# Feed-forward blocks of a streaming encoder: high and low x as one moving operand of 1152 columns, in pieces of 384

## The reference, cut to what matters

```python
def sq_relu_ffn(x, w1, w2):                       # w1 1024 x 4096, w2 4096 x 1024
    return jnp.square(jax.nn.relu(x @ w1)) @ w2
...
        x = layer_norm(DN_ALPHA * x + mix, ln1_g[i], ln1_b[i])
        x = layer_norm(DN_ALPHA * x + sq_relu_ffn(x, ffn_w1[i], ffn_w2[i]), ln2_g[i], ln2_b[i])
```

## Time and profile before

| | |
|---|---|
| median of 3 runs | 1731.77 us (1729.48 to 1733.89) |
| the profiled execution | 1733.15 us |
| its span, first to last instruction | 1731.4 us |
| PE busy, share of the span | 1698.0 us, 98% |
| DVE, POOL, ACT busy | 959.6, 910.5, 463.5 us |
| granted TensorE clock, mean | 0.994 |

### The profile page before, as it was taken

One profiled execution on the slowest core, in us unless ns is written; L12 is line 12 of the kernel. 1 busy time (PEld: TensorE's weight loads), 2 busy tenths in 40 slices (PEclk: granted clock), 3 DMA queues, 4 the chain that ended last, 5 costly groups with the idle time before them and its releaser, 6 DMA issues.

```text
span 1731.4 us, 31956 instructions
## 1 busy us (share of the span) xinstructions
PE 1698.0 (98%) x12276; PEld 1631.5 (94%) x12276; DVE 959.6 (55%) x1657; ACT 463.5 (27%) x812; POOL 910.5 (53%) x744
## 2 busy tenths in 40 slices
PE   7999999999999999999999899999999999999996
PEld 7899999999999999999999777999999999999996
DVE  7799999998846451222315822887355431312226
ACT  2344334444213440211202511211024320302105
POOL 6454344444455555555555555445555565555552
PEclk9999999999999999999999999999999999999998
DMA  4223222233122222222222222122222222222221
GB/s 171 80 98 98 98 95 83 79 98 108 59 87 77 82 85 85 77 82 86 85 82 77 94 100 73 65 78 66 86 74 86 84 75 85 85 85 75 84 86 67
DMA packets 45564, 148.03 MB, mean 85 GB/s; under 512 B 7200, under 2 KB 12704, under 8 KB 44320
## 3 DMA queue, kind: packets, MB, share of 16 engines
q1 hardware_dynamic: 37456, 131.09, 22.7%
q10 hardware_dynamic: 8016, 15.59, 2.8%
HBM read 141.50 MB, written 5.15 MB: 85 GB/s over the span
## 4 chain that ended last, share of the span: by engine, by line
PE 70%; DVE 2%; ACT 1%; issue 0%; ACTq 0%; DVEq 0%
PE ps L581 21%; PE ps L582 21%; PE ps L583 21%; PE ps L826 2%; PE ps L827 2%; PE ps L828 2%; PE ps L867 1%; DVE s L1568 0%; PE ps L868 0%; DVE hl L1668 0%; DVE r L1662 0%; PE ps L869 0%; DVE vm L1853 0%; ACT r L1150 0%; DVE na L1723 0%
## 5 line engine op out<-in xcount | busy, mean ns | idle before, releaser
L510 POOL TENSOR_TENSOR wl<-wraw,wh 128x1024 fp32r<-128x1024 f32 x240 | 590.1, 2459 | 20.0
L581 PE MATMUL ps<-xh,wh 128*128 128x288 f32 (+1 forms) x1968 | 588.3, 299 | 9.4 <-DVE xl L1268 9.4
L582 PE MATMUL ps<-xl,wh 128*128 128x288 f32 (+1 forms) x1968 | 585.2, 297 | 0.0
L583 PE MATMUL ps<-xh,wl 128*128 128x288 f32 (+1 forms) x1968 | 585.1, 297 | 0.0
L581 PE MATMUL ps<-hh,wh 128*128 128x288 f32 x1632 | 482.6, 296 | 0.0
L583 PE MATMUL ps<-hh,wl 128*128 128x288 f32 x1632 | 480.8, 295 | 0.0
L582 PE MATMUL ps<-hl,wh 128*128 128x288 f32 x1632 | 480.5, 294 | 0.0
L507 POOL TENSOR_TENSOR tick<-tick 128x1 f32<-128x1 f32 x240 | 59.3, 247 | 761.9 <-DMA wraw<-wstream 761.9
L581 PEld LDWEIGHTS ps<-xh,wh 128*128 128x128 f32 x1968 | 374.3, 190 | 10.1 <-DVE wl L1265 7.9
L583 PEld LDWEIGHTS ps<-xh,wl 128*128 128x128 f32 x1968 | 373.2, 190 | 0.0
L582 PEld LDWEIGHTS ps<-xl,wh 128*128 128x128 f32 x1968 | 372.9, 189 | 0.2
(11 more groups left out here) (226 smaller groups left out, 1713.5 us busy)
## 6 DMA issues: line engine op xcount, KB each, us to landing
wraw<-wstream SPq DMA_DIRECT2D x241, 512.0 KB, 3.4
acb<-acum_scratch ACTq DMA_DIRECT2D x8, 1152.0 KB, 6.1
xr<-x SPq DMA_DIRECT2D x4, 576.0 KB, 7.2
out_y<-r SPq DMA_DIRECT2D x8, 288.0 KB, 2.2
hs<-ssm_in ACTq DMA_DIRECT2D x8, 128.0 KB, 5.8
out_ssm_s<-hsn ACTq DMA_DIRECT2D x8, 128.0 KB, 5.0
out_ssm_p<-hp ACTq DMA_DIRECT2D x8, 128.0 KB, 1.9
bb<-bias_v ACTq DMA_DIRECT2D x1, 1024.0 KB, 4.9
```

What stands on the lines that cost most here:

```text
L510: pool.tensor_tensor(m.wl[:, s], m.wraw[:, s], m.wh[:, s], ALU.subtract).then_inc(S.w_ready, 1)
L581: mm(out, w_hi, x[0], start=start, stop=False)
L582: mm(out, w_hi, x[1], start=False, stop=False)
L583: return mm(out, w_lo, x[0], start=False, stop=stop)
```

## The change

High and low x are laid out side by side in one tensor (`x2`, `h2`), so that a matmul can run from the end of the high part on into the low part. For each step k of a unit there are five matmuls in place of six (`wide_products`): with the high weights over high and low x (1152 columns, 1156 in an up block) in pieces of 384, of 2 x 192 (2 x 194 in an up block: the rest of the high part and the beginning of the low part, to two places of one bank) and of 384; then with the low weights over high x in pieces of 384 and 192 (194). The number of columns is the same. A slot takes three banks (0 to 2, or 3 to 5); the columns of the high product lie side by side in it, and those of the low product too, and the one who empties it adds both: two DVE operations in place of one in a down block (`wide_add`), and in an up block two and a small one for the extra columns (`cda` on ACT, `cd` on DVE). The units that run in halves (the first of a feed-forward, the last two or four) keep the three matmuls of 288 columns; `residual_add` stays for the units outside the feed-forwards. Sums over the partitions move to other banks, and after the first unit the PE waits for `d_mean`, since the next unit writes the banks that the sums are in.

```diff
-        self.xh_ext = put("xh", [P, KT, TX], F32R)
-        self.xl_ext = put("xl", [P, KT, TX], F32R)
+        self.x2_ext = put("x2", [P, 2, KT, TX], F32R)
+        self.xh_ext = self.x2_ext[:, 0]
+        self.xl_ext = self.x2_ext[:, 1]
...
-        self.hh = put("hh", [P, 16, T], F32R)
-        l0 = self.at
-        self.hl = put("hl", [P, 16, T], F32R)
+        l0 = h0 + 16 * T * 4
+        self.h2 = put("h2", [P, 2, 16, T], F32R)
+        self.hh = self.h2[:, 0]
+        self.hl = self.h2[:, 1]
...
+def half_bank(n, s, h):
+
+    return (3 if n % 2 else 2) * s + h
+
+
+def first_bank(n, s, h):
+
+    return (2 if n == 1 else 3) * s + h
+
+
+def sum_banks(n):
+
+    return (4, 6) if n == 1 else (0, 6)
+
+
+def wide_slot(m, s):
+
+    return m.ps[:, 3 * s:3 * s + 3, :].rearrange("p b t -> p (b t)")
+
+
+def high_part(m, s, n=T):
+
+    at = 512 - WIDE
+    return wide_slot(m, s)[:, at:at + n]
...
+def low_part(m, s, width, n=T):
+
+    at = 1024 - (width - WIDE)
+    return wide_slot(m, s)[:, at:at + n]
...
+def twice(ap, step):
+
+    return bass.AP(tensor=ap.tensor, offset=ap.offset, ap=[ap.ap[0], (step, 2), ap.ap[1]])
...
+    def wide_products(s, w, k, x):
+
+        w_hi, w_lo = m.wh[:, w, k * P:(k + 1) * P], m.wl[:, w, k * P:(k + 1) * P]
+        n = x.shape[-1] - WIDE
+        first, last = k == 0, k == KT - 1
+        head, tail, low = m.ps[:, 3 * s, 512 - WIDE:512], m.ps[:, 3 * s + 1, 0:n], m.ps[:, 3 * s + 2, 0:WIDE]
+        x_head, x_tail = x[:, 0, k, 0:WIDE], x[:, 0, k, WIDE:WIDE + n]
+        mm(head, w_hi, x_head, start=first, stop=False)
+        mm(twice(tail, 512 - n), w_hi, twice(x_tail, x[:, :, k, :].ap[1][0] - WIDE), start=first, stop=False)
+        mm(low, w_hi, x[:, 1, k, n:n + WIDE], start=first, stop=last)
+        mm(head, w_lo, x_head, start=False, stop=last)
+        return mm(tail, w_lo, x_tail, start=False, stop=last)
+
+    def wide_unit(u, w, turn, x):
+
+        pe.wait_ge(S.w_ready, u + 1)
+        wait(pe, m.slot_evac[w % 2], turn)
+        for k in range(KT):
+            last = wide_products(w % 2, w, k, x)
+        last.then_inc(S.gemm_done, 1)
...
-        run_few(u0 + 1, 3, m.xh_ext, m.xl_ext, ext_half)
-        run(u0 + 4, 3, m.xh_ext, m.xl_ext, ext_half)
+        pe.wait_ge(S.d_mean, n + 1)
+        wide_few(u0 + 1, 3, m.x2_ext)
+        wide_run(u0 + 4, 3, m.x2_ext)
...
-                    run(u0 + 8 * b, 2, m.hh[:, k:k + 8], m.hl[:, k:k + 8])
+                    wide_run(u0 + 8 * b, 2, m.h2[:, :, k:k + 8])
...
-                run(u0 + 8 * b, 2, m.xh_ext, m.xl_ext, ext_half)
+                wide_run(u0 + 8 * b, 2, m.x2_ext)
...
-        f(m.msq[:, :, :], m.ps[:, 4:6, 0:HT], ACT.Square, scale=1.0 / D).then_inc(S.d_msq, 1)
-        f(m.mean[:, :, :], m.ps[:, 4:6, 0:HT], ACT.Copy, scale=1.0 / D).then_inc(S.d_mean, 1)
+        sums = m.ps[:, sum_banks(n)[0]:sum_banks(n)[0] + 2, 0:HT]
+        f(m.msq[:, :, :], sums, ACT.Square, scale=1.0 / D).then_inc(S.d_msq, 1)
+        f(m.mean[:, :, :], sums, ACT.Copy, scale=1.0 / D).then_inc(S.d_mean, 1)
...
+    def up_tile(layer, u, c, i, j):
+
+        before = 32 * layer + 8 * c + j
+        act.wait_ge(S.gemm_done, 2 * i + (u + 1))
+        if before % 32 == 0 and isinstance(i, int):
+            f(m.cd[:, j], m.ps[:, first_bank(2 * layer, u % 2, 1), HT:HT + 2], ACT.Copy).then_inc(S.cd_ready, 1)
+        else:
+            f(m.cda[:, j], ext_columns(high_part(m, u % 2, TX)), ACT.Copy).then_inc(S.cd_a, 1)
...
+    def wide_add(u0, i, j, turn, k=None):
+
+        u = u0 + j
+        s = u % 2
+        r = one(m.r, 2 * i + j if k is None else k)
+        dve.wait_ge(S.gemm_done, 2 * i + (u + 1))
+        dve.wait_ge(m.slot_evac[1 - s], i + (slot_turn(u - 1) + 1))
+        tt(r, high_part(m, s), r, ALU.add).then_inc(S.add_a, 1)
+        dve.wait_ge(S.add_a, 2 * i + turn)
+        tt(r, low_part(m, s, T), r, ALU.add).then_inc(m.slot_evac[s], 1)
...
+            if n == 1:
+                wide_add(u, 0, 0, 24 + k + 1, k)
...
+            wide_add(u, 0, 0, 54 + k + 1, k)
...
-        dve.wait_ge(S.cd_ready, 2 * i + (done + 1))
+        s = u % 2
         if done >= 2 or not isinstance(i, int):
             dve.wait_ge(S.rl_ready, 2 * i + (done - 1))
-        stt(halves(ta), m.mean[:, :, :], m.cd[:, j, 0:1], bank_pair(m, u % 2), ALU.mult, ALU.subtract
-            ).then_inc(m.slot_evac[u % 2], 1)
+        if done % 32 == 0 and isinstance(i, int):
+            dve.wait_ge(S.cd_ready, done + 1)
+            bank = first_bank(2 * layer, s, 0)
+            stt(halves(ta), m.mean[:, :, :], m.cd[:, j, 0:1], m.ps[:, bank:bank + 2, 0:HT], ALU.mult, ALU.subtract
+                ).then_inc(m.slot_evac[s], 1)
+        else:
+            mean = m.mean[:, :, :].rearrange("p h t -> p (h t)")
+            dve.wait_ge(S.cd_a, 2 * i + (done - layer))
+            tt(m.cd[:, j], m.cda[:, j], ext_columns(low_part(m, s, TX, TX)), ALU.add).then_inc(S.cd_ready, 1)
+            dve.wait_ge(S.cd_ready, 2 * i + (done + 1))
+            stt(ta, mean, m.cd[:, j, 0:1], high_part(m, s), ALU.mult, ALU.subtract).then_inc(S.up_a, 1)
+            dve.wait_ge(S.up_a, 2 * i + (done - layer))
+            tt(ta, ta, low_part(m, s, TX), ALU.subtract).then_inc(m.slot_evac[s], 1)
...
```

More of the change, by code:

```diff
@@ L17 @@
 HT = T // 2
+WIDE = 384
 TX = T + 2
@@ L337, in __init__ @@
         self.cd = put("cd", [P, 2, 2], offset=t0 + 25 * row + 128)
+        self.cda = put("cda", [P, 2, 2], offset=t0 + 25 * row + 192)
         self.dbias = put("dbias", [P, EARLY], offset=t0 + 25 * row + 160)
@@ L583, in products, with wide_few, wide_run @@
         return mm(out, w_lo, x[0], start=False, stop=stop)
+    def wide_products(s, w, k, x):
[15 more added lines that the diff above has]
+        last.then_inc(S.gemm_done, 1)
+    def wide_few(u0, n, x):
+        for u in range(u0, u0 + n):
+            wide_unit(u, u % RING, slot_turn(u), x)
+    def wide_run(u0, n, x):
+        with pe.Fori(0, n) as i:
+            for j in range(RING):
+                wide_unit(4 * i + (u0 + j), (u0 + j) % RING, 2 * i + slot_turn(u0 + j), x)
     def unit(u, w, turn, xh, xl, half=half_of):
@@ L608, in deferred_sums, with last_block @@
             pe.wait_ge(S.sum1_ready, 10 * n + 8 + 2 * h)
[L609 removed]
+            mm(m.ps[:, sum_banks(n)[0] + h, 0:HT], m.ones[:, :], m.s1[:, h], start=True, stop=True)
             pe.wait_ge(S.sum2_ready, 10 * n + 8 + 2 * h)
[L611 removed]
+            last = mm(m.ps[:, sum_banks(n)[1] + h, 0:HT], m.ones[:, :], m.s2[:, h], start=True, stop=True)
         last.then_inc(S.d_sums, 1)
[L614 to L616 removed]
+    def last_block(n, u0, xh, xl, wide=None):
+        if wide is None:
+            run_few(u0, 6, xh, xl)
+        else:
+            wide_few(u0, 6, wide)
         for h in range(2):
@@ L1129, in mean_squared @@
             act.wait_ge(S.end_stat, h + 1)
-            f(m.msq[:, h], m.ps[:, 4 + h, 0:HT], ACT.Square, scale=1.0 / D).then_inc(S.end_msq, 1)
-            f(m.mean[:, h], m.ps[:, 4 + h, 0:HT], ACT.Copy, scale=1.0 / D).then_inc(S.end_mean, 1)
+            f(m.msq[:, h], m.ps[:, END_SUM_BANK[h], 0:HT], ACT.Square, scale=1.0 / D).then_inc(S.end_msq, 1)
+            f(m.mean[:, h], m.ps[:, END_SUM_BANK[h], 0:HT], ACT.Copy, scale=1.0 / D).then_inc(S.end_mean, 1)
         def deviation(h):
@@ L1170, in end_norm, with residual_tile, up_pair @@
             affine(1, pair)
+    def up_tile(layer, u, c, i, j):
[5 more added lines that the diff above has]
+            f(m.cda[:, j], ext_columns(high_part(m, u % 2, TX)), ACT.Copy).then_inc(S.cd_a, 1)
+        act.wait_ge(S.t_ready, 2 * i + (before + 1))
+        f(m.rl[:, j], m.ta[:, j], ACT.Relu, bias=m.cd[:, j, 1:2], scale=-1.0).then_inc(S.rl_ready, 1)
+        act.wait_ge(S.rl_ready, 2 * i + (before + 1))
+        if before >= 2 or not isinstance(i, int):
+            act.wait_ge(S.hid_lo, 2 * i + (before - 1))
+        f(m.hq[:, j], m.rl[:, j], ACT.Square).then_inc(S.hid_ready, 1)
+        f(one(m.hh, 2 * i + (8 * (c % 2) + j)), m.rl[:, j], ACT.Square).then_inc(S.hid_hi, 1)
+    def residual_tile(layer, c, i):
+        gain, bias = (m.again[:, layer, i + at:i + at + 1] if isinstance(i, int) else m.again[:, layer, bass.ds(i + at, 1)]
+                      for at in (4 * c, KT + 4 * c))
+        act.wait_ge(S.gain_ready, layer + 1)
+        act.wait_ge(S.rn_centred, i + (8 * layer + 4 * c + 1))
+        f(one(m.r, i + 4 * c), one(m.r, i + 4 * c), ACT.Identity, bias=bias, scale=gain).then_inc(S.rn_ready, 1)
+    def up_pair(layer, u, c, i):
+        up_tile(layer, u, c, i, 0)
+        up_tile(layer, u + 1, c, i, 1)
+        if c < 2:
+            residual_tile(layer, c, i)
     def ffn(layer, u0):
@@ L1174, in ffn @@
             if kind == "up":
[L1175 to L1193, removed]
+                up_pair(layer, u0 + 8 * b, c, 0)
+                with act.Fori(1, 4) as i:
+                    up_pair(layer, u0 + 8 * b, c, i)
     act.wait_ge(S.tail_out, 16)
@@ L1793, in ffn @@
             else:
```

(2 more changed lines are left out.)

57 lines of the change are left out of this document (33 added, 24 removed).

## The result

| | before | changed |
|---|---|---|
| median | 1732.05 us (4 runs) | 1746.51 us (4 runs, 1743.11 to 1748.04) |
| ratio to the kernel before | | 1.0074, 95% interval 1.0062 to 1.0086 |
| span of the profiled execution | 1731.4 us | 1745.0 us |
| PE instructions, as many loads | 12276 | 11316 |
| between the statistics' last sums: first feed-forward | 412.27 us | 418.95 us |

A forecast was written before the change was run, and what follows sets the result against it. PE-bound: matmuls in flight 98% of the span, each with an overhead. Up steps +3.4 us, down steps +2.4 us, path +0.5: in all +6.3, 1739.5 for the profiled execution, median 1738.1 us; range 1731 to 1752.

The forecast's parts named there:

- The short piece: Last matmul of each five-matmul step, 192 or 194 columns: costs a weight load, about 111 ns, not 93.
- the hidden load: Rival: the weight load hides behind the 192-column matmul, which then costs 93 ns; 1721 us in all; chance 0.13.
- Plain float32 rate for a short float32r matmul: Rival: the last matmul of a step takes 323 ns, 212 more than forecast; 1942 us in all; chance 0.04.
- The sign that I had set for a failure: In the PE timeline: the prediction fails if the distance after the 192-column matmul is under 0.10 us.
- The long pieces: Four matmuls per step, 384 columns (down) or 388 (up): 173.5 or 175.2 ns each, 694.0 or 695.7 together.
- the two places: Second matmul of a step, two stretches of 192 columns: extra cost taken as 0; 12.5 us if each stretch paid a start.
- The price of the steps before: Six matmuls of a step k in the old feed-forwards: 6 x 133.3 = 799.8 ns, for down and up blocks alike.
- the 13 ns over the columns: Overhead of each feed-forward matmul beyond its columns' time, 13.1 to 14.0 ns, taken as nearly independent of width.
- overheads add: Rival: 13 ns follow the load too (124 ns), or two stretches pay a second start; 1750.6 us; chance 0.09.
- 109 to 112: Rounding range in ns of the 192-column matmul's 111: 109 takes 1.9 us off the total, 112 adds 1.
- Slots, new wait, other banks, POOL, DMA: Work beside the feed-forward matmuls: later slot emptying, PE's wait for `d_mean`, moved sums, POOL's split, DMA queue; all hidden, 0.
- The place on the path: End of the first feed-forward's last block, DVE nearly full: a second addition delays the sums, +0.5 us taken.

## Why the prediction was right, and where its sizes were off

**The short piece** was forecast at 111 ns (bounds 93 and 124) and measured 108.5 in a down block and 109.5 in an up block. The step that led there, that only one set of weights can wait and that a load takes 0.11 us, held in all kernels, whatever the order and the width. Its rival, the hidden load, is out. So is the Trainium skill's sentence ("TensorE: Matmul & The Clock Gate", section "Architectural detail: the array is 16× 32×32, not 1× 128×128") in the use that I had given it as a rival: a matmul here may begin before its load's record of 0.19 us has ended, but not sooner than 0.108 us after it began, and that is too late to hide a load behind 192 columns. Plain float32 rate for a short float32r matmul is out too.

The sign that I had set for a failure was badly chosen. It was a distance under 0.10 us after the short matmul, and the recorded starts are 0.09 us apart (690.05 and 690.14). Taken by its letter it says that the load hides. Only the longer record of the next matmul and the starts of the loads show the 0.11, as at L581 in the earlier trace rows, so the sign should have named the loads.

**The long pieces** were forecast at 173.5 and 175.2. In down blocks they are 173.5 to 176: nearly right, and the two places cost nothing there (174, beside 173.5 to 176 for pieces with one). In up blocks they are 175 to 179.5, 1.5 to 6 ns each over the line. This term was mis-sized: an up step came to 821 for 806.7. Those 14 ns x 496 are 7.0 us, more than the whole forecast; the down steps, 807 for 805, add 1.0 us. Why the up steps are so dear stays open: they took 823 ns with x padded, 820 with the weights moved and 821 without the second DVE operation.

**The price of the steps before** was one mean for both kinds, 799.8 ns. It is 795 for h and 805 for x. For the up steps that took 5 off, for the down steps it added 5; over 496 and 464 steps the two errors cancel but for 0.3 us. Together: the forecast 5.2 and 6.9 ns per step became 12 and 16. 464 x (12 - 5.2) + 496 x (16 - 6.9) ns = 3.2 + 4.5 = 7.7 us, which is what lies between 5.8 us forecast and 13.5 measured by steps. Behind the sizes is one assumption, that the 13 ns over the columns belong to a matmul as such. They are 10 to 24 ns in the kernels here (322 columns at 144 ns and 512 in two places at 237, both in up blocks with x padded), and part of that moves with the place of the operands. The split of the windows by kind of block would have shown beforehand that steps of x are dearer.

**The range** (1731 to 1752) was carried by the bounds "overheads add" and "109 to 112"; the measured 1746.5 lies between forecast and that rival, but not by its mechanism: the overhead did not come on top of the load. So the direction and its cause were forecast, the size came out twice as large (13.35 us for 6.3), and that the range still holds it is luck.

**Slots, new wait, other banks, POOL, DMA**: forecast 0, measured 0.03 us for the second read, which is under what the stretches tell apart, and no new wait of the PE. The place on the path at the end of the first feed-forward was forecast at +0.5; the additions there do come later (DVE, changed kernel):

```profile
943.91 0.76 DVE L1662 TENSOR_TENSOR r<-ps,r 128x576 f32<-128x576 f32 x1 [2.66 <-PE ps L647]
944.70 0.76 DVE L1664 TENSOR_TENSOR r<-ps,r 128x576 f32<-128x576 f32 x1
...
949.00 2.66 DVE L1688 TENSOR_TENSOR s<-s,sqm 128x288 f32<-128x288 f32 x1
...
956.66 0.46 DVE L1737 TENSOR_TENSOR r<-ps,r 128x288 f32<-128x288 f32 x1 [0.43 <-PE ps L634]
...
958.40 2.62 DVE L1682 TENSOR_TENSOR s<-s,r 128x288 f32<-128x288 f32 x1
```

DVE still has 0.43 us of idle time ahead of the last addition (0.36 before), so the second addition was swallowed, and the two feed-forwards lose the same, 6.68 and 6.67 us, though the second has no such place. The term was 0.

## What to carry to other kernels

Before cutting matmuls into fewer and unequal pieces, look for the shortest piece: where every matmul loads its own weights, one shorter than a load costs the load, and what the others gain in overhead is gone (here 13 ns gained, 16 lost). The loss doesn't show at the short matmul but as a longer duration of the one behind it, so compare durations of equal shapes, and read the loads beside the matmuls. And a price per instruction that was fitted over two layouts is good to a few ns only; with 960 steps of five matmuls, 2 ns are 10 us.

## What the runs showed of the hardware that was not expected

The price of a float32r matmul depends on where its moving operand starts, and on where the weights lie, and it repeats as if with a period of 256 or 512 bytes: the same 40 matmuls took steps of 798 to 838 ns at rows of 2312 bytes, 820 to 826 at 2368, all 807 at 2304; with rows of 2304 bytes and the cut at 352 odd and even k alternate between 784 and 790. Two columns of difference in the cut (322 to 320) were worth 12 ns per step of 807, by address, width or place in PSUM. What meets in the memory was not settled.
